# Half 1's differential softmax mix: from VectorE to scaled diagonals (ScalarE) and accumulating products (TensorE)

## The reference

```
a1 = softmax(q1 k1 * scale + bias);  a2 = softmax(q2 k2 * scale + bias)
a  = a1 - lam * a2
out = a @ v
```

## Time and profile before

| | |
|---|---|
| median of 3 runs | 817.4 us (816.75 to 818.07) |
| the profiled execution | 817.13 us, its span 815.3 us |
| PE busy | 675.8 us (83%) |
| DVE busy | 526.1 us (65%) |
| ACT busy | 236.8 us (29%) |
| POOL busy | 500.6 us (61%) |
| DMA | 297.92 MB, mean 365 GB/s over the span |
| chain that ended last | DMA 46%, PE 31%, POOL 9%, issue 5%, ACT 4%, DVE 4% |

### The profile page before, as it was taken

How to read it: one execution, slowest core, us unless ns; L and a number is a source line. 1 busy time by engine, 2 the same in 40 slices (tenths; PEclk the granted TensorE clock), 3 DMA queues, 4 the chain that set the end, 5 groups by cost and what they waited for, 6 DMA issues and landing times.

```text
span 815.3 us, 7481 instructions
## 1 busy us (share of the span) xinstructions
PE 675.8 (83%) x2205; PEld 366.0 (45%) x2205; DVE 526.1 (65%) x1389; ACT 236.8 (29%) x606; POOL 500.6 (61%) x533
## 2 busy tenths in 40 slices
PE   5998997799959978789998888887777778886665
PEld 4887676565434434345544444433323323332221
DVE  5575168869826666666666766676767667665454
ACT  6657344443105241311213131331212121202110
POOL 5011007677757777777777777677767777777650
PEclk9999998699979999999999999999999998889999
DMA  9944418999999999999999999999999999999994
GB/s 327 323 156 165 145 52 315 348 368 409 409 395 395 403 410 408 410 408 410 408 410 409 409 409 409 411 409 409 409 410 408 410 409 410 409 409 410 408 410 174
DMA packets 92153, 297.92 MB, mean 365 GB/s; under 512 B 8769, under 2 KB 17106, under 8 KB 92114
## 3 DMA queue, kind: packets, MB, share of 16 engines
q0 software_dynamic: 73728, 268.47, 83.1%
q1 hardware_dynamic: 18386, 28.98, 10.4%
HBM read 296.36 MB, written 1.05 MB: 365 GB/s over the span
## 4 chain that ended last, share of the span: by engine, by line
DMA 46%; PE 31%; POOL 9%; issue 5%; ACT 4%; DVE 4%; DVEq 0%; SPq 0%; POOLq 0%; ACTq 0%
DMA v_row<-in_peer_v_dram,expert 28%; DMA u_row<-in_peer_u_dram,expert 15%; PE bank L1418 14%; POOL u_row L482 5%; PE xg L1166 4%; PE bank L1291 3%; PE bank L1337 3%; POOL v_row L494 3%; DMA wq<-in_peer_w_query_dram 2%; DVE u_row L1065 2%; PE bank L1232 1%; PE bank L1215 1%; ACT soft L586 1%; PE bank L1166 1%; DMA x_sb<-in_x_dram 0%
## 5 line engine op out<-in xcount | busy, mean ns | idle before, releaser
L1418 PE MATMUL bank<-v_row,diag 128*128 128x512 f32 x1000 | 478.3, 624 | 108.3 <-DMA v_row<-in_peer_v_dram,expert 93.3
L1065 DVE CUSTOM_DVE_ANT_0 u_row<-u_row,xg 128x1024 f32<-128x1024 f32 x244 | 296.2, 1220 | 182.3 <-DMA u_row<-in_peer_u_dram,expert 174.9
L1418 PEld LDWEIGHTS bank<-v_row,diag 128*128 128x128 f32 x1000 | 190.1, 199 | 352.1 <-issue 320.1
L482 POOL DMA_INDIRECT u_row<-in_peer_u_dram,expert x256 | 244.1, 953 | 134.3 <-issue 58.0
L494 POOL DMA_INDIRECT v_row<-in_peer_v_dram,expert x256 | 241.7, 944 | 104.6 <-issue 64.8
L737 ACT ACTIVATE h_gelu<-h_dot 128x4 f32<-128x4 f32 x64 | 12.8, 202 | 249.5 <-DVE h_dot L1065 249.4
L744 ACT ACTIVATE diag<-ident,act_w 128x128 f32<-128x128 f32 x250 | 82.7, 389 | 3.6 <-DVE act_w L1078 3.6
L1337 PEld LDWEIGHTS bank<-featT,wq 128*128 128x128 f32 x384 | 48.2, 199 | 21.7 <-issue 11.1
L1337 PE MATMUL bank<-featT,wq 128*128 128x128 f32 x384 | 48.7, 283 | 10.6 <-DMA wq<-in_peer_w_query_dram 9.7
L697 ACT ACTIVATE qT<-bank 128x128 f32<-128x128 f32 x32 | 8.9, 278 | 160.7 <-PE bank L1337 160.7
L388 POOL TENSOR_TENSOR normed<-qk_raw,t_qk_rs 128x512 f32<-128x512 f32 x4 | 4.1, 1047 | 57.7 <-DVE t_qk_rs L938 57.7
(11 more groups left out here) (164 smaller groups left out, 554.0 us busy)
## 6 DMA issues: line engine op xcount, KB each, us to landing
w_raw<-in_w_in_dram SPq DMA_DIRECT2D x12, 1024.0 KB, 7.8
wq<-in_peer_w_query_dram SPq DMA_DIRECT2D x6, 1024.0 KB, 22.5
w_raw<-in_w_out_dram SPq DMA_DIRECT2D x4, 1024.0 KB, 5.2
u_row<-in_peer_u_dram,expert POOLq DMA_INDIRECT x256, 20.6
v_row<-in_peer_v_dram,expert POOLq DMA_INDIRECT x256, 20.7
x_sb<-in_x_dram SPq DMA_DIRECT2D x2, 512.0 KB, 3.6
wq_high<-in_peer_w_query_dram SPq DMA_DIRECT2D x1, 768.0 KB, 9.3
g_row<-in_norm_g_dram SPq DMA_DIRECT2D x1, 512.0 KB, 13.1
```

What stands on the lines that cost most here:

```text
L482: pool.indirect_dma_start(u_rows[n % U_RING][:, :], None, peer_u[0], bass.IndirectOffsetOnAxis(ap=expert[:, u, s:s + 1], axis=0))\
L1065: dve.tensor_tensor_reduce(out=row[:, :], in0=row[:, :], in1=x_of, scale=1.0, scalar=0.0, op0=ALU.mult, op1=ALU.add, accum_out=h_dot[:, u ...
L1418: ins = mm(ps[y_bank(h, c)][:, :], diag[:, m % DIAG_RING, :], v_row(n)[:, c * COLS:(c + 1) * COLS], start=False, stop=True, skip_group_che ...
```

## The change

Half 1's two mixes are no longer formed by DVE. DVE computes only the two columns of factors, 1/sum1 and now -lambda/sum2 (`mix_weights`). ACT writes them out as scaled diagonals, identity times a column: four 128 x 128 blocks per mix, into the tile `mixed` that held the mix before (`scale_diagonals`). PE then multiplies each 128 x 128 block of both softmaxes by its diagonal and sums the two in PSUM: 8 products where there were 4 transposes (`folded_transposes`). Half 0's mix stays on DVE (`mix_first`), with the sign moved into the factor.

```diff
-MIXES_READY = {0: 1, 3: 2, 4: 3}
-MIX_AFTER = {0: 0, 4: 1, 6: 4}
+FOLDED = {3: 4, 4: 6}
+FOLD_AFTER = {4: 1, 6: 4}
...
+            def scale_diagonals(b):
+                h, wide, _, first = batch(b)
+                act.wait_ge(weights_ready, (b - 2) // 2)
+                act.wait_ge(probsT_done, FOLD_AFTER[b])
+                c, r = h * INSTANCES + first, 4 * h + (first - MOBA_HEADS) // 2
+                for t in range(wide):
+                    for second, by in enumerate((tiny["rsum"][:, c + 2 * t:c + 2 * t + 1], tiny["rlam"][:, r + t:r + t + 1])):
+                        at = slice((2 * t + second) * P, (2 * t + second + 1) * P)
+                        ins = act.activation(mixed[:, at], ident[:, :], ACT.Copy, scale=by)
+                ins.then_inc(scales_ready, 1)
...
             exponentials(5)
+            scale_diagonals(4)
             act.wait_ge(late_v_done, 1)
...
             exponentials(7)
+            scale_diagonals(6)
             probs_evac(4)
...
-            def mix_diff(b):
+            def mix_weights(b):
                 dve.wait_ge(exp_done, b + 2)
-                need(dve, probsT_done, MIX_AFTER[b])
                 link(dve.reciprocal(tiny["rsum"][:, c:c + 2 * wide], tiny["sums"][:, c:c + 2 * wide]))
...
+                return dve.tensor_scalar(tiny["rlam"][:, r:r + wide], tiny["rsum"][:, c + 1:c + 2 * wide:2], tiny["lam"][:, 1:2],
+                                         -1.0, ALU.mult, ALU.mult)
...
-            mix_diff(4)
+            mix_weights(4).then_inc(weights_ready, 1)
             bias_and_max(6)
             bias_and_max(7)
-            mix_diff(6)
+            mix_weights(6).then_inc(weights_ready, 1)
...
+            def folded_transposes(s):
+                b = FOLDED[s]
+                pe.wait_ge(exp_done, b + 2)
+                pe.wait_ge(scales_ready, s - 2)
+                for t in range(4):
+                    cols = slice(t * P, (t + 1) * P)
+                    for second in range(2):
+                        scale = mixed[:, (2 * (t // 2) + second) * P:(2 * (t // 2) + second + 1) * P]
+                        ins = mm(ps[PROBS_BANK[s]][:, cols], soft[:, (b + second) % 4, cols], scale,
+                                 start=second == 0, stop=second == 1)
+                ins.then_inc(probsT_done, 1)
...
-            mixed_transposes(3)
+            folded_transposes(3)
...
-            mixed_transposes(4)
+            folded_transposes(4)
```

More of the change, by code:

```diff
@@ L291, in layer @@
         mixed_ready = sem("mixed_ready")
+        weights_ready = sem("weights_ready")
+        scales_ready = sem("scales_ready")
         probsT_done = sem("probsT_done")
@@ L873, in mix_diff, with mix_first @@
                 dve.wait_ge(exp_done, b + 2)
-                need(dve, probsT_done, MIX_AFTER[b])
                 link(dve.reciprocal(tiny["rsum"][:, c:c + 2 * wide], tiny["sums"][:, c:c + 2 * wide]))
                 r = 4 * h + (first - MOBA_HEADS) // 2
-                link(dve.tensor_scalar(tiny["rlam"][:, r:r + wide], tiny["rsum"][:, c + 1:c + 2 * wide:2], tiny["lam"][:, 1:2],
-                                       None, ALU.mult))
-                cols = soft_cols(b)
+                return dve.tensor_scalar(tiny["rlam"][:, r:r + wide], tiny["rsum"][:, c + 1:c + 2 * wide:2], tiny["lam"][:, 1:2],
+                                         -1.0, ALU.mult, ALU.mult)
+            def mix_first():
+                _, wide, _, first = batch(0)
+                link(mix_weights(0))
+                cols = soft_cols(0)
                 for t in range(wide):
-                    second = soft[:, (b + 1) % 4, cols[t]]
-                    at = mark(dve.tensor_scalar(second, second, tiny["rlam"][:, r + t:r + t + 1], None, ALU.mult))
+                    second = soft[:, 1, cols[t]]
+                    at = mark(dve.tensor_scalar(second, second, tiny["rlam"][:, t:t + 1], None, ALU.mult))
                 dve.wait_ge(dve_step, at)
                 for t in range(wide):
-                    ins = dve.scalar_tensor_tensor(mixed[:, cols[t]], soft[:, b % 4, cols[t]],
-                                                   tiny["rsum"][:, c + 2 * t:c + 2 * t + 1], soft[:, (b + 1) % 4, cols[t]],
-                                                   ALU.mult, ALU.subtract)
+                    ins = dve.scalar_tensor_tensor(mixed[:, cols[t]], soft[:, 0, cols[t]],
+                                                   tiny["rsum"][:, first + 2 * t:first + 2 * t + 1], soft[:, 1, cols[t]],
+                                                   ALU.mult, ALU.add)
                 ins.then_inc(mixed_ready, 1)
@@ L949, in _ @@
                     link(dve.tensor_scalar(tiny["lam"][:, 1:2], tiny["lam"][:, 0:1], LAM_INIT, None, ALU.add))
-                    mix_diff(0)
+                    mix_first()
                 if j == 10:
@@ L1189, in logits, with mixed_transposes @@
                 ins.then_inc(logits_done, 1)
-            def mixed_transposes(s):
-                pe.wait_ge(mixed_ready, MIXES_READY[s])
+            def mixed_transposes():
+                pe.wait_ge(mixed_ready, 1)
                 for t in range(4):
-                    ins = pe.transpose(ps[PROBS_BANK[s]][:, t * P:(t + 1) * P], mixed[:, t * P:(t + 1) * P], ident[:, :])
+                    ins = pe.transpose(ps[PROBS_BANK[0]][:, t * P:(t + 1) * P], mixed[:, t * P:(t + 1) * P], ident[:, :])
+                ins.then_inc(probsT_done, 1)
[9 more added lines that the diff above has]
+                                 start=second == 0, stop=second == 1)
                 ins.then_inc(probsT_done, 1)
@@ L1258, in _ @@
                 if j == 8:
-                    mixed_transposes(0)
+                    mixed_transposes()
                 if j == 9:
```

## The result

| | kernel before | changed kernel |
|---|---|---|
| median | 817.31 us (20 executions) | 821.2 us (20 executions) |
| lowest to highest | 814.35 to 818.23 | 817.6 to 822.71 |
| ratio | | 1.0043, 95% interval 1.0031 to 1.0055 |
| profiled execution, span | 817.13, 815.3 | 818.44, 816.7 |
| DVE / ACT / PE busy | 526.1 / 236.8 / 675.8 us | 522.4 / 238.8 / 678.3 us |

The changed kernel is slower by 0.43% (3.5 us; 2.5 to 4.5); the two medians lie 3.9 us apart. DVE lost 3.7 us of busy time and the kernel is not faster for it. The executions of the changed kernel don't scatter, they stand in groups: seven between 817.6 and 818.75, three between 819.9 and 820.31, ten between 822.09 and 822.71. The median of 821.2 is the middle between 820.31 and 822.09: no execution lies there.

A forecast was written before the change was run, and what follows sets the result against it. The PE and ACT chain releasing POOL's gathers was taken to set the end, through transfers idle at 152 to 172 us. Terms 0.4 + 1.4 + 0.9 = 2.7 us, adjusted for clock to +2.3, gave 819.5 us, range 816.5 to 821.8.

The forecast's parts named there:

- The end follows the second unit's first gather: Gathers at 152 to 172 us: delayed releases of POOL lengthen the transfers' idle time and move the end equally, +2.3 us.
- The rival that queued gathers hide the delay: Transfers at 152 to 172 us: gathers already queued outlast the later releases, so nothing moves, 817.4 us; chance 0.10.
- The other release that I named: Fifth v gather at 150.18 us, released by PE's last values; predicted 2.3 us later, like the second unit's gather.
- The terms of the chain: Half 1: +0.4 us first pair's diagonals on ACT, +1.4 its products on PE, +0.9 second pair's mix; 2.7 us longer.
- dearer products: Rival on PE: accumulating products with different stationary blocks stall between, +3.8 us on the 2.7, 823.6 us; chance 0.05.
- DVE's saved 3 us would shorten nothing: Half 1's mixes: DVE's busy time falls by about 3 us and no wait shortens by it.
- The clock's term: PE's clock around `folded(4)`: sum 1.4 us if full, 4.4 if halved through its products; +2.3 chosen between.
- my rival's condition: Holding-clock rival: PE at full clock from 138 to 142 us, shortening that stretch to give 815.7 us.
- its own signs: Wrong if exponentials 6 start as before, the transfers' share doesn't fall, or PE's clock is 1.00 behind 138 us.
- the rival's case: PE's clock holds and stays up through the next stretch, 815.7 to 818.7 us; chance 0.27.
- the forecast's case: Longer chain of PE and ACT delays POOL's releases, +1.6 to +4.5 us, 818.7 to 821.9 us; chance 0.58.

The follow-up runs named there:

- e12: Only the second pair (batches 6 and 7) over diagonals, PE's four later stands and an early stand in half 0 filled; median 815.8 us, ratio 0.9982 to the kernel before.
- e10: Changed kernel with eight extra ACT activations ahead of exponentials 8, lengthening PE's stand behind `key_transposes(3)`; median 822.81 us, ratio 1.0065 to the kernel before.
- e9: Changed kernel run a third time, unchanged, for another profile; median 820.6 us, ratio 1.0048 to the kernel before; profiled execution 819.95 us, in the middle group.
- e7: Changed kernel run again, unchanged, for another profile; median 818.99 us, ratio 1.0033 to the kernel before; profiled execution 818.01 us, in the lower group.
- e1: Only the first pair (batches 4 and 5) over diagonals, batches 6 and 7 mixed on DVE as in the kernel before; median 819.6 us, ratio 1.0023 to it.
- e2: Only the second pair (batches 6 and 7) over diagonals, batches 4 and 5 mixed on DVE; median 816.9 us, ratio 0.9997 to the kernel before.
- e3: Changed kernel with the copy of v ahead of the first pair's diagonals in ACT's list; median 821.86 us, ratio 1.0050 to the kernel before.
- e4: Changed kernel with 17 filler products of unused result in PE's four stands; median 816.93 us, ratio 0.9997 to the kernel before.
- e5: Kernel before with filler products in its own PE stands (6, 2, 6 and 1); median 816.93 us, ratio 1.0001 to the kernel before.
- e6: Kernel before with eight extra ACT activations (1.26 us) ahead of `d_squares(1)`; median 818.17 us, ratio 1.0015 to the kernel before.
- e8: Only the second pair over diagonals, with PE's four later stands filled; median 817.02 us, ratio 1.0003 to the kernel before.
- e11: Kernel before with seven filler products in PE's stand in half 0 (62.9 to 64.9 us); median 815.82 us, ratio 0.9988 to the kernel before.

## Why the prediction was right

**The end follows the second unit's first gather, one for one: right.** Over the 14 profiles of all kernels that gather was issued between 155.40 us (e12) and 162.37 us (e10), and the execution's time is 659.2 to 660.7 us more than that in every one (a straight line through the 14 has a slope of 0.96):

| profile | first gather | gelu | second unit's first gather, released by | time |
|---|---|---|---|---|
| before | 122.91 | 151.53 | 157.78, DVE's experts | 817.13 |
| changed | 123.62 | 152.51 | 158.57, DVE's experts | 818.44 |
| e9 (changed) | 123.06 | 154.32 | 160.57, DVE's experts | 819.95 |
| e7 (changed) | 123.51 | 152.70 | 158.76, DVE's experts | 818.01 |
| e1 first pair | 123.27 | 154.26 | 160.70, DVE's experts | 820.00 |
| e2 second pair | 122.18 | 148.08 | 155.57, issue | 815.35 |
| e3 v copy first | 123.40 | 152.26 | 158.32, DVE's experts | 817.99 |
| e4 changed, filled | 123.82 | 151.59 | 157.85, issue | 817.37 |
| e5 before, filled | 123.49 | 150.66 | 157.71, issue | 817.05 |
| e6 before, 1.3 us on ACT | 122.35 | 151.43 | 157.51, DVE's experts | 817.43 |
| e8 second pair, filled | 124.31 | 150.68 | 158.15, issue | 818.32 |
| e10 longer stand | 123.81 | 156.11 | 162.37, DVE's experts | 822.38 |
| e11 early filler | 122.24 | 149.71 | 155.90, DVE's experts | 815.06 |
| e12 second pair, all filled | 121.83 | 147.93 | 155.40, issue | 816.05 |

The rival that queued gathers hide the delay is out for delays. For gains there is something like it, which I had not: POOL's own issuing of 24 gathers holds the second unit's first one, however early its experts are. The other release that I named, the fifth v gather behind the last values, was PE's only in the profiles of the kernel before, e9 and e10; elsewhere POOL's list held that gather too.

**The terms of the chain: right.** 0.4, 1.4 and 0.9 were forecast, 0.3, 1.35 and 0.9 read in the profile. The factor of four from the Trainium skill (TensorE: Matmul & The Clock Gate, section Terms) would have made the first pair's eight products 3.6 us; they took 1.95 at the full clock, so the row was the right source, and "dearer products" is out. That DVE's saved 3 us would shorten nothing held for the changed kernel. It does not hold for the second pair alone: from the first gather to the end of the last maxima e2 takes 18.9 us and e5, with the mix on DVE, 19.7, although e2's `values(4, 6)` start 1.2 us later. With the full clock DVE comes onto this chain, and its second mix with it.

**The clock's term: the mis-sized one.** I took 2.3 us, a value between a sum of 1.4 with the clock held and 4.4 with it halved through `folded(4)` and after. The measured 3.5 us (2.5 to 4.5) lie inside my range and nearer its upper side. Some of that is luck: ten of the 20 executions lie above the range's end of 821.8, and with one more in the upper group the median would have too. Two things were wrong in it. First, the two halves of that term do not go together: in all four profiles of this chain (the changed kernel, e3, e7 and e9) `folded(4)` ran mostly at half clock (3.36, 3.55, 3.65 and 3.40 us), while `values(4, 6)` behind it had the full one (1.16); that makes the chain 2.7 + 1.4 - 1.3 = 2.8 us longer up to that point. Second, I wrote that all behind it runs "as before, at half clock from 138.3 to 155.3 us". That was one execution's state, not the kernel's. In the changed kernel it is full in some executions (the lower group) and half in others, 2.4 us apart. In the lower group both my rival's condition (full clock behind 138 us) and the longer chain hold, and they cancel almost; in e9 nothing cancels. The terms are also counted against a single profile of the kernel before: by e6's and e11's, with `values(4, 6)` in 1.17 and 1.16 us, the -1.3 was within its reach already.

**By its own signs the forecast failed in the profiled execution.** I had written that the prediction is wrong if the share of transfers in the gap doesn't fall or if PE's clock is 1.00 behind 138 us. Both came: the share rose from 0.90 to 0.94, and the clock was 0.99. That execution is the rival's case, with +1.3 us. In e9 the share fell to 0.86, the clock was 0.54 and the time +2.8: that is the forecast's case. The median over the groups came where the forecast had it, but not as one kernel in one state.

**What made it slower, then.** Each step of the chain is longer by its own length (e1, and the terms above), and the clock adds to that or takes it back. With the stands filled the gelu comes 1.1 us sooner behind the first gather than in the lower group and 3.5 us sooner than in the middle one, and the loss in time is gone (e4). The fillers change the clock and nothing that the chain has to do, so the granted clock around stands of PE carries most of the loss, and these stands are longer because the steps before them are (e2's is 1.38 us, with both pairs it is 2.41). With only one of the two pairs changed the loss is 1.9 us or none; with both it is 3.5. That e4 ends level with the kernel before does not mean that the instructions are free: at the filled kernels' 817 us POOL's list holds, and it covers the 1.4 us by which e4's chain is longer than e8's. How the 3.5 us divide between clock and instructions in the time itself can't be told with these runs.

**Left open.** What the 822.3 group is, half of all executions: the two states of the clock that were seen fall 0.8 to 1.8 us short of it. Why some u and v gathers take 2.0 us to issue and not 0.94, and two of the first 20 in one profile and four in another, which by itself moves POOL's list by 2 us. What the kernel before would take with the full clock throughout, since e5 did not hold it.

## What to carry to other kernels

Work moved off an engine that waits anyway buys nothing: follow the chain first, in each state of the clock that profiles show (here VectorE was off the chain at the half clock and on it at the full one), and count for the new path every hand-over (factors on DVE, diagonals on ACT, products on PE), none of which overlaps the next. Where a chain has stands of TensorE like those here (1.4 to 2.9 us), one profile shows one state of the clock; look at the list of execution times for groups, and take a second and a third profile, of the kernel before as well, before a "runs at half clock" goes into a sum. Filler products into a free PSUM bank are a cheap test of how much of a difference is the clock's, as long as nothing else then holds the end: look which release comes last in the filled kernel.

## What was not expected of the hardware

- The same stands of PE, 2.41 us before the same eight products and 1.75 us before the later transposes, were followed by full or by half clock in the later stretch in different executions of one program (0.99 and 0.54); a stand of 2.04 us in half 0 left the clock at 1.00 in e9 and was followed by 0.70 at 64 to 66 us and 0.60 at 65 to 69 us in the changed kernel's first profile. The 24 products behind that stand took 7.33 us there and 5.72 in the kernel before.
- Real products at 128 x 128 cost 0.24 us and transposes 0.11: a factor of two, in float32.
- Small activations in a row overlap: eight of 128 x 64, 0.24 us long each, took 1.26 us together.
- Filling an early stand of 2 us, 57 us ahead of the first gather, moves the end of an 817 us kernel by 1 us (e11; 0.1 to 1.8).
